# Layer 2 normalizes its attention scores instead of its queries, and the second block's attention runs its last eight units one step later

## The chip, the cores and the metric

The kernel runs on one core of a Trainium2 chip. The metric is the device time of one launch in microseconds; the number given for a kernel is the median of its runs.

## What is computed

Two transformer-like blocks in float32 over 512 tokens of width 1024. The first block has four layers with residual sums; its second layer ("layer 2" here, `mixer_b`) is a dilated window attention. The second block begins with a differential attention over 512 tokens and 256 context tokens. These two are touched:

```python
def mixer_b(h, w_in, q_gain, k_gain, w_out):
    ...
    for g, (window, dilation) in enumerate(B_PATTERNS):     # 3 groups, 8 heads of 128
        q = apply_partial_rotary(rms_norm(qkv[:, :, 0, g], q_gain[g]), cos, sin)
        k = apply_partial_rotary(rms_norm(qkv[:, :, 1, g], k_gain[g]), cos, sin)
        o, lse = dilated_window_attention(q, k, qkv[:, :, 2, g], window // dilation, dilation)
    ...
    y = o.reshape(bsz, S, B_WIDTH) * jax.nn.silu(z)
    return y @ w_out

def diff_attend(q, k, v, lam):                              # 8 heads, 2 maps each
    s = jnp.einsum("bqhpd,bkhpd->bhpqk", q, k) * (HEAD_DIM_2 ** -0.5)
    p = jax.nn.softmax(s, axis=-1)
    a = p[:, :, 0] - lam * p[:, :, 1]
    return jnp.einsum("bhqk,bkhe->bqhe", a, v)
```

`rms_norm` divides by the root of the mean square over a head's 128 features. The partial rotary turns the first 32 features.

## The kernel before

The program is written by hand, engine by engine: `pe_program`, `act_program`, `dve_program`, `pool_program` and `sp_program` each issue their instructions in the order of the code, and semaphores (`wait_ge`, `then_inc`) join them. An engine runs its list strictly in order, so a wait holds up all that stands behind it. Nothing schedules; the order of the loops is the order on the chip. In the names, T and X count TensorE's events, A ScalarE's, V VectorE's and G GpSimd's.

**Products.** A product with a weight keeps float32 accuracy through three matmuls of type fp32r (`mm3`, lines 547 to 549): high part by high part, high by low, low by high. A weight panel is 128 by 2048 float32. SP loads it into one of three slots (`Wr`), ScalarE rounds it to `Wh` (line 1322), GpSimd subtracts to get `Wl` (line 355, four pieces), and `ahead` on both engines does this for the panel two further on. A plain float32 matmul, as for sums of squares, is one instruction that the profile records twice.

**Layer 2.** Features lie on partitions, tokens on columns. For each pair of heads `i` (4 of them) TensorE makes 12 tiles of queries and keys, `t` = 4*group + 2*(key) + head, each of 24 matmuls of 512 columns, then six value tiles, two gate tiles and eight units `u` of attention. After each tile comes `ssq` of the tile before (line 792): a float32 matmul of all ones by the squares, so that each token's sum stands on all 128 partitions. ScalarE squares the tile (line 1518), copies it (line 1523) and takes the root of the sums (line 1510). In `rest`, VectorE inverts the 128x512 roots (line 2133), multiplies tile, gain and inverse (line 2138), swaps halves of 32 rows (line 2147) and multiplies by the sine table (line 2149). GpSimd's `rope` multiplies by the cosine (line 409) and adds (line 412), for queries and keys alike.

A unit is 128 queries by 512 keys: four small matmuls and two large ones into PSUM (lines 832 and 834); VectorE adds the mask and takes the row's maximum in one pass (line 2163) and scales it (line 2166); ScalarE exponentiates (line 1536); VectorE divides (lines 2170 and 2172); TensorE transposes (`flip`, line 843) one unit later; then the products with the values (lines 856 and 863). Each of units 0 to 3 stands behind a value tile, units 4 and 6 behind a gate tile, units 5 and 7 behind none.

**The output projection of layer 2** begins in the last units' tail (`part_out`). ScalarE's `out` first squares two finished output tiles (line 1379), which wait for VectorE's residual sums (line 1967), and then rounds the panel two ahead.

**The second block's attention.** 32 units `g` of 128 queries, eight heads of four. `step(n)` on TensorE issues the scores of unit n+1 (line 1080), the transposes of unit n (`flip`, lines 1090 and 1095) and the product with the values of unit n-1 (line 1111). VectorE's step is `combine(n)` (lines 2348 and 2350), `maxima(n+1)` (lines 2333 and 2335), a copy of two transposed blocks (line 2386) and `weights(n+1)` (lines 2340 and 2342); ScalarE copies the other four blocks (line 1739) and exponentiates both maps (line 1715). The scores of a unit fill PSUM banks 4 to 7, so those of n+1 wait for the exponentials of n. Up to n = 23 each step also holds a projection tile of some 5.8 us. From n = 24 there is none: from n = 25 a step holds two matmuls of a filter (`filt`, line 1150, through PSUM bank 3), which VectorE multiplies (lines 2360 to 2364) and GpSimd adds (lines 454 and 455). After each head come `sums` (line 643), a root, `spread` (line 648) and a scaled copy (lines 2398 and 2002). Then `first_out` starts the output projection.

Of the kernel before, what the change touches and what calls it, by code (L numbers as in the profile page):

```python
# [116 lines left out]

def near_keys(ap, t):

    return ap.rearrange("a (r q n) -> a q r n", r=4, q=4)[:, t:t + 2]  # L120
# [8 lines left out]
D_UNITS = D_HEADS * TT  # L129
FILTER_AT = {25 + 4 * half + t: (half, t) for half in range(2) for t in range(TT)}  # L130
# [67 lines left out]
def setting(nc, ctx, I):  # L198
# [19 lines left out]
    E.ones, E.ident = sb("ones", [P, P]), sb("ident", [P, P])  # L218
# [6 lines left out]
    E.rc = sb("rc", [P, 2, TT])  # L225
    E.rs = sb("rs", [P, 2, S])
    E.sq = sb("sq", [P, 2, S])
# [9 lines left out]
    with ExitStack() as over:  # L237
# [8 lines left out]
            ("stB", [P, B_UNITS, 4], F32), ("PTB", [P, 4, 512], F32), ("szB", [P, S], F32))  # L246
# [15 lines left out]
    E.dlF, E.woF, E.decF, E.kcF = phase(("dlF", [P, D], F32), ("woF", [64, 2 * D], F32), ("decF", [P, 2, S], F32), ("kcF", [P, 2, 2, 512], F32))  # L262
# [17 lines left out]
D_FIRST = [0, 1, 2, 4, 3, 5, 6, 7]  # L280

# [63 lines left out]
def pool_program(E, pool):  # L345
# [39 lines left out]
    def mixer_b():  # L385
        norm("B", E.Ah, E.Al)
        for i in range(4):
            t = 0
            for g in range(3):
                for qk in range(2):  # L390
                    for f in range(2):
                        if t:
                            rope(i, t - 1)
                        if f == 0:
                            ahead("B", "qk", i, g, qk)
                        t += 1
            for g in range(3):
                ahead("B", "v", i, g)
                if g == 0:
                    rope(i, 11)  # L400
            ahead("B", "z", i)
        out("B", 0)

    def rope(i, t):
        g, qk, f = t // 4, t // 2 % 2, t % 2
        q = (E.KB if qk else E.QB)[0:32, g, f, :]
# [121 lines left out]
def pe_program(E, pe):  # L528
# [255 lines left out]
    def mixer_b():  # L784
# [3 lines left out]
        def ssq(i, t):  # L788
            r = t % 2
            into(4 + r)  # L790
            pe.wait_ge(*A.of("B", "sq", i, t))
            pe.matmul(psx[:, r, :], ones[:], sq[:, r, :], start=True, stop=True).then_inc(*X.did("B", "ssq", i, t))  # L792
            emptied[4 + r] = A.of("B", "sqrt", i, t)

        def qk(i, t):
# [11 lines left out]
            if t:  # L807
                ssq(i, t - 1)
# [15 lines left out]
        def scores(i, u):  # L824
# [3 lines left out]
            if r == 0:  # L828
                pe.wait_ge(*G.of("B", "rope", i, 10 + hh))
# [60 lines left out]
        for i in range(4):  # L890
# [5 lines left out]
            ssq(i, 11)  # L896
# [136 lines left out]
    def attention():  # L1033
# [119 lines left out]
        def step(n, f):  # L1153
            if f:
                filt(*f, 0)
            if n + 1 < D_UNITS:
                scores(n + 1)
            if n < D_UNITS:
                flip(n)
            if 1 <= n <= D_UNITS:  # L1160
                values(n - 1)
            if f:
                filt(*f, 1)
            if n >= 5 and (n - 2) % TT == 3:
                sums((n - 2) // TT)
            if n >= 6 and (n - 3) % TT == 3:
                spread((n - 3) // TT)
# [7 lines left out]
        for n in range(D_UNITS + 1):  # L1175
# [137 lines left out]
def act_program(E, act):  # L1313
# [51 lines left out]
    def out(L, half, squares, src, before):  # L1365

        for n in range(4):
            beside = L == "A3" and half
            if beside and n < 2:
                context(n)  # L1370
            if n == 3 and squares and not beside:
# [11 lines left out]
            ahead(L, "o", half, n)  # L1383
# [111 lines left out]
    def mixer_b():  # L1495
        PB, stB, ropeB = E.PB, E.stB, E.ropeB
        qf = E.QB[:].rearrange("p a b n -> p (a b n)")
# [3 lines left out]
        act.dma_start(qf[:, 0:4 * 512], I["k_maskB"]).then_inc(*LDB.did(0))  # L1501
# [3 lines left out]
        def sqrt(i, t):  # L1505
            r = t % 2
            act.wait_ge(*X.of("B", "ssq", i, t))
            if t >= 2:
                act.wait_ge(*V.of("B", "qk", i, t - 2))
            act.activation(rs[:, r, :], psx[:, r, :], ACT.Sqrt, bias=eps[:, 0:1], scale=1.0 / P).then_inc(*A.did("B", "sqrt", i, t))  # L1510

        def qk(i, t):
            act.wait_ge(*T.of("B", "qk", i, t))
            if t >= 2:
# [1136 lines left out]
```

## Time and profile before

| | |
|---|---|
| median of 3 runs | 3177.42 us (3175.05 to 3180.74) |
| the profiled execution, its own time | 3173.78 us |
| its span | 3171.9 us |
| TensorE busy | 3097.2 us, 98% of the span |
| VectorE, GpSimd, ScalarE busy | 1577.5, 1552.7, 1099.8 us |
| mean granted clock of TensorE | 0.992 of full speed |

The profile is one execution. Busy time of TensorE counts from the start of a matmul to a modelled end, and ends of neighbours overlap, so that the time one matmul takes from the others is read from the distance between starts and not from its duration. An idle time is shown with what ended it.

### The profile page before, as it was taken

How to read it: one execution, taken by the hardware profiler on the slowest of the kernel's cores; microseconds unless marked ns; L12 is line 12 of the kernel's file. 1: busy time of each engine (PE TensorE's matmuls, PEld its weight loads, DVE VectorE, ACT ScalarE, POOL GpSimd, SP SyncE). 2: the span in 40 equal slices, each digit the busy share in tenths (PEclk: the TensorE clock that was granted, in tenths of full speed). 3: DMA queues.
4: the chain of work that ended last, by engine and by line, in shares of the span. 5: the costliest groups of instructions: out<-in, count | busy, mean ns of one | idle time of the engine just before them, and what ended most of it. 6: DMA issues, size and time to landing. Idle time of an engine off the chain costs nothing.

```text
span 3171.9 us, 38137 instructions
## 1 busy us (share of the span) xinstructions
PE 3097.2 (98%) x15692; PEld 2524.8 (80%) x15692; DVE 1577.5 (50%) x2066; ACT 1099.8 (35%) x1445; POOL 1552.7 (49%) x1138
## 2 busy tenths in 40 slices
PE   8999999999999999999999999899999999999998
PEld 6888878788887888878887888666888777778887
DVE  6654474838473525355456777644211356542113
ACT  3322244444443423332223444434222343242222
POOL 4444475748473555454434422235544565355444
PEclk9999999999999999999999999999999999999999
DMA  5544322222222323355443111112223242222331
GB/s 199 171 151 159 133 93 70 80 67 80 67 80 68 105 93 95 109 187 176 137 160 116 54 41 41 41 54 93 93 94 106 81 146 81 79 68 93 97 103 67
DMA packets 270975, 319.24 MB, mean 101 GB/s; under 512 B 6851, under 2 KB 228690, under 8 KB 270483
## 3 DMA queue, kind: packets, MB, share of 16 engines
q1 hardware_dynamic: 232768, 247.48, 24.2%
q10 hardware_dynamic: 38034, 69.34, 6.4%
q8 instruction: 124, 2.03, 0.3%
q14 instruction: 49, 0.39, 0.0%
HBM read 310.50 MB, written 6.29 MB: 100 GB/s over the span
## 4 chain that ended last, share of the span: by engine, by line
PE 92%; DVE 4%; ACT 1%; POOL 1%; issue 1%; DMA 1%; ACTq 0%; SPq 0%; DVEq 0%
PE ps L547 26%; PE ps L549 25%; PE ps L548 25%; PE psx L792 1%; PE psx L1080 1%; PE ps L1111 1%; PE ps L618 1%; PE psx L771 1%; POOL Wl L355 1%; PE psx L1234 1%; PE ps L586 1%; DVE stD L2333 1%; PE psx L834 1%; PE ps L582 1%; PE ps L583 1%
## 5 line engine op out<-in xcount | busy, mean ns | idle before, releaser
L355 POOL TENSOR_TENSOR Wl<-Wr,Wh 128x512 fp32r<-128x512 f32 x928 | 1269.7, 1400 | 1415.7 <-ACT Wh L1322 1411.5
L547 PE MATMUL ps<-Ah,Wh 128*128 128x512 f32 x1944 | 778.1, 400 | 0.0
L549 PE MATMUL ps<-Ah,Wl 128*128 128x512 f32 x1944 | 757.5, 390 | 0.0
L548 PE MATMUL ps<-Al,Wh 128*128 128x512 f32 x1944 | 757.3, 390 | 0.0
L1322 ACT ACTIVATE Wh<-Wr 128x2048 fp32r<-128x2048 f32 x232 | 443.0, 1909 | 354.7 <-DMA Wr<-in_w_mlp_in_dram 110.2
L547 PEld LDWEIGHTS ps<-Ah,Wh 128*128 128x128 f32 x1944 | 365.1, 188 | 84.9 <-issue 12.0
L547 PE MATMUL ps<-Yh,Wh 128*128 128x512 f32 x1088 | 426.8, 392 | 5.2 <-POOL Wl L355 5.2
L548 PEld LDWEIGHTS ps<-Al,Wh 128*128 128x128 f32 x1944 | 365.2, 188 | 82.1 <-issue 8.9
L549 PEld LDWEIGHTS ps<-Ah,Wl 128*128 128x128 f32 x1944 | 364.9, 188 | 77.0
L548 PE MATMUL ps<-Yl,Wh 128*128 128x512 f32 x1088 | 424.5, 390 | 0.0
L549 PE MATMUL ps<-Yh,Wl 128*128 128x512 f32 x1088 | 424.3, 390 | 0.0
L547 PEld LDWEIGHTS ps<-Yh,Wh 128*128 128x128 f32 x1088 | 205.1, 188 | 50.0 <-POOL Wl L355 5.6
L549 PEld LDWEIGHTS ps<-Yh,Wl 128*128 128x128 f32 x1088 | 204.9, 188 | 42.9
L548 PEld LDWEIGHTS ps<-Yl,Wh 128*128 128x128 f32 x1088 | 205.0, 188 | 42.2
L547 PE MATMUL ps<-Wh,Ah 128*128 128x256 f32 (+1 forms) x688 | 220.7, 321 | 2.1 <-DVE vA L2057 2.1
L548 PE MATMUL ps<-Wl,Ah 128*128 128x256 f32 (+1 forms) x688 | 215.1, 313 | 0.0
L549 PE MATMUL ps<-Wh,Al 128*128 128x256 f32 (+1 forms) x688 | 215.0, 313 | 0.0
L2049 DVE SCALAR_TENSOR_TENSOR macc<-modw,sc,macc 128x512 f32<-128x512 f32 x168 | 158.4, 943 | 111.1 <-DMA modw<-in_w_mod_dram 104.6
L2133 DVE RECIPROCAL rs<-rs 128x512 f32<-128x512 f32 x48 | 160.6, 3346 | 38.9 <-ACT rs L1510 38.9
L2410 DVE TENSOR_TENSOR tmp<-tmp 128x512 f32<-128x512 f32 x64 | 52.3, 817 | 201.2 <-ACT tmp L1786 201.2
L547 PEld LDWEIGHTS ps<-Wh,Ah 128*128 128x128 f32 x688 | 131.1, 191 | 13.8 <-issue 4.3
L548 PEld LDWEIGHTS ps<-Wl,Ah 128*128 128x128 f32 x688 | 131.1, 191 | 9.2 <-issue 1.9
(404 smaller groups left out, 3895.6 us busy)
## 6 DMA issues: line engine op xcount, KB each, us to landing
Wr<-in_a_w_in_dram SPq DMA_DIRECT2D x48, 1024.0 KB, 6.6
modw<-in_w_mod_dram ACTq DMA_DIRECT2D x96, 512.0 KB, 5.5
Wr<-in_b_w_in_dram SPq DMA_DIRECT2D x40, 1024.0 KB, 5.0
Wr<-in_w_mlp_in_dram SPq DMA_DIRECT2D x32, 1024.0 KB, 5.5
Wr<-in_w_mlp_out_dram SPq DMA_DIRECT2D x32, 1024.0 KB, 5.1
Wr<-in_a_w_out_dram SPq DMA_DIRECT2D x16, 1024.0 KB, 5.1
Wr<-in_c_w_in_dram SPq DMA_DIRECT2D x16, 1024.0 KB, 5.5
Wr<-in_attn_w_qkv_dram SPq DMA_DIRECT2D x12, 1024.0 KB, 5.1
```

What stands on the lines that cost most here:

```text
L355: last = pool.tensor_tensor(E.Wl[:, s, part], E.Wr[:, s, part], E.Wh[:, s, part].bitcast(F32), ALU.subtract)
L547: pe.matmul(o, ah, bh, start=first, stop=False)
L548: pe.matmul(o, ah, bl, start=False, stop=False)
L549: return pe.matmul(o, al, bh, start=False, stop=last)
L582: pe.matmul(bank[b], part(E.Wh, p, k, f * P, f * P + P, KD), Ah[:, k, :], start=(k == 0), stop=False)
L583: pe.matmul(bank[b], part(E.Wl, p, k, f * P, f * P + P, KD), Ah[:, k, :], start=False, stop=False)
L586: m = pe.matmul(bank[b], part(E.Wh, p, k, f * P, f * P + P, KD), Al[:, k, :], start=False, stop=(k == KD - 1))
L618: pe.matmul(bank[t], Ah[:, a, t * P:(t + 1) * P], part(W, p, k, 0, S, TT), start=(a == 0 and W is E.Wh), stop=False)
L1322: act.activation(E.Wh[:, s, :], E.Wr[:, s, :], ACT.Copy).then_inc(*HI.did(p))
L2049: dve.scalar_tensor_tensor(t, w, E.sc2[:, k, who:who + 1], t, ALU.mult, ALU.add).then_inc(*V.did("mac", L, nb, who, k))
L2133: dve.reciprocal(rs[:, r, :], rs[:, r, :]).then_inc(*V.did())
L2410: dve.tensor_tensor(t, t, t, ALU.mult).then_inc(*V.did(L, "sqr", iq, c))
```

## The change

**Early rounding.** In ScalarE's `out` of layer 2 the first `ahead` stands ahead of the first two squares.

**Queries of layer 2.** ScalarE writes the tile times its gain straight into `QB`. The sums of squares of both heads' query tiles come from eight float32 matmuls of 32 output rows and 128 columns, ScalarE takes roots of 128x256, TensorE transposes them in two 128x128 blocks, so that a token's root stands in a column, and VectorE inverts four columns of each. The scores are multiplied by that column in the pass that adds the mask, which is now three instructions (one per group of the three attentions) and a maximum of its own. The rotation of queries is wholly on VectorE: shuffle, two products, one sum, of 32 rows each.

**Keys of layer 2.** Squares are rounded by ScalarE to `rsR`, VectorE takes the rest `sqR`, and the sum is two fp32r matmuls. Roots, 128x512 inverses, gain and rotation stay as before.

**Later order.** From unit 24 on, the transposes of unit n-1 and the values of n-2 stand in step n; VectorE's step begins with `maxima(n+1)`, and `combine(n)` comes after the first filter product. From unit 25 the second map's weights alternate between two buffers. There is one more step, and the two last heads' sums come one step later.

The core of the diff:

```diff
+D_LAST = 24
+def is_key(t):
+    return t // 2 % 2 == 1
+def second(E, g):
+    return E.p1E[:] if g > D_LAST and g % 2 else E.p1D
+def behind(h):
+    return 1 if 4 * h >= D_LAST else 0
...
 # pe_program, mixer_b
-        def ssq(i, t):
-            r = t % 2
-            into(4 + r)
-            pe.wait_ge(*A.of("B", "sq", i, t))
-            pe.matmul(psx[:, r, :], ones[:], sq[:, r, :], start=True, stop=True).then_inc(*X.did("B", "ssq", i, t))
+        def key_sum(i, t):
+            b = 5 - t % 2
+            into(b)
+            pe.wait_ge(*V.of("B", "sl", i, t))
+            pe.matmul(bank[b], E.onesR[:], E.rsR[:, t % 2, :], start=True, stop=False)
+            pe.matmul(bank[b], E.onesR[:], E.sqR[:, t % 2, :], start=False, stop=True).then_inc(*X.did("B", "ssq", i, t))
+        def query_sums(i, g):
+            into(4)
+            pe.wait_ge(*A.of("B", "sq", i, 4 * g + 1))
+            for f in range(2):
+                for q in range(TT):
+                    m = pe.matmul(psx[32 * q:32 * q + 32, 0, f * P:(f + 1) * P], ones[:, 0:32], sq[:, f, q * P:(q + 1) * P], start=True, stop=True)
+        def columns(i, g):
+            pe.wait_ge(*A.of("B", "sqrt", i, 4 * g))
+            for f in range(2):
+                m = pe.transpose(psx[:, 0, (2 + f) * P:(3 + f) * P], rs[:, 1, f * P:(f + 1) * P], ident[:])
-            if t:
-                ssq(i, t - 1)
+            if t % 4 == 2:
+                query_sums(i, t // 4)
+            elif t % 4 == 3:
+                key_sum(i, t - 1)
+                columns(i, t // 4)
+            elif t % 4 == 0 and t:
+                key_sum(i, t - 1)
...
 # dve_program, mixer_b
+        def turn_query(i, t):
+            q, swapped = QB[0:32, t // 4, t % 2, :], PB[0:32, 0, :]
+            dve.wait_ge(*A.of("B", "cp", i, t))
...
+            dve.stream_shuffle(swapped, q, SWAP).then_inc(*V.did())
+            dve.tensor_tensor(swapped, swapped, ropeB[:, 1, :], ALU.mult).then_inc(*V.did())
+            dve.tensor_tensor(q, q, ropeB[:, 0, :], ALU.mult).then_inc(*V.did())
+            dve.tensor_tensor(q, q, swapped, ALU.add).then_inc(*V.did("B", "turned", i, t))
...
-            dve.tensor_tensor_reduce(PB[:, u % 2, :], psx[:, u % 2, :], maskB[:, u % 4, :], 1.0, 10 * NEG,
-                                     ALU.add, ALU.max, stB[:, u, 0:1]).then_inc(*V.did("B", "sc", i, u))
+            for g, c0, c1 in ((0, 0, 256), (1, 256, 384), (2, 384, 512)):
+                dve.scalar_tensor_tensor(PB[:, u % 2, c0:c1], psx[:, u % 2, c0:c1], rq(g, u // 4)[:, u % 4:u % 4 + 1], maskB[:, u % 4, c0:c1],
+                                         ALU.mult, ALU.add).then_inc(*V.did("B", "sc", i, u))
+            dve.tensor_reduce(stB[:, u, 0:1], PB[:, u % 2, :], AX.X, ALU.max).then_inc(*V.did("B", "mx", i, u))
...
-            for t in range(11):
-                rest(i, t)
+            for t in range(13):
+                if t % 4 == 3:
+                    rate(i, t // 4)
+                if t < 12:
+                    if is_key(t):
+                        square_low(i, t)
+                    else:
+                        turn_query(i, t)
+                if t and is_key(t - 1):
+                    scaled(i, t - 1)
+                    turn_key(i, t - 1)
...
 # act_program, out
+            if L == "B" and n == 0:
+                ahead(L, "o", half, n)
...
-            ahead(L, "o", half, n)
+            if L != "B" or n:
+                ahead(L, "o", half, n)
...
 # pe_program, attention
         def step(n, f):
+            late = n >= D_LAST
+            if n + 1 < D_UNITS:
+                scores(n + 1)
             if f:
                 filt(*f, 0)
-            if n + 1 < D_UNITS:
-                scores(n + 1)
-            if n < D_UNITS:
+            if not late:
                 flip(n)
-            if 1 <= n <= D_UNITS:
+            elif D_LAST <= n - 1 < D_UNITS:
+                flip(n - 1)
+            if 1 <= n <= D_LAST:
                 values(n - 1)
+            elif D_LAST <= n - 2 < D_UNITS:
+                values(n - 2)
             if f:
                 filt(*f, 1)
...
 # dve_program, attention: the order within a late step
+            if late and n + 1 < D_UNITS:
+                maxima(n + 1)
...
+            g = n - 1 if late else n
...
             if n in FILTER_AT:
                 filt(*FILTER_AT[n], 0)
+            if late and n < D_UNITS:
+                combine(n)
+            if n in FILTER_AT:
+                filt(*FILTER_AT[n], 1)
             if n + 1 < D_UNITS:
                 weights(n + 1)
```

**How the order moves.** On TensorE, layer 2, head pair 0, behind a tile. Before, the float32 sum:

```order
L548 MATMUL ps<-Al,Wh 128x512
L549 MATMUL ps<-Ah,Wl 128x512
L792 MATMUL psx<-sq,ones 128x512
L547 MATMUL ps<-Ah,Wh 128x512
L548 MATMUL ps<-Al,Wh 128x512
```

and now, behind the second key tile of a group:

```order
L567 MATMUL ps<-Al,Wh 128x512
L568 MATMUL ps<-Ah,Wl 128x512
L811 MATMUL psx<-rsR,onesR 128x512
L812 MATMUL psx<-sqR,onesR 128x512
L827 MATMUL psx<-ident,rs 128x128 x2
L566 MATMUL ps<-Ah,Wh 128x512
```

The one float32 sum became two fp32r matmuls, and the transposes of the queries' roots stand behind them. Behind the first key tile of a group stand the eight small matmuls (line 820) instead, behind the next group's first query tile the two of the second key tile, and behind a second query tile nothing.

On ScalarE, where layer 2's output projection begins (`Wh` is a rounded weight panel). Before:

```order
L1598 ACTIVATE Yh<-sq 128x512
L1546 ACTIVATE PTB<-psx 128x512 x2
L1598 ACTIVATE Yh<-szB 128x512
L1379 ACTIVATE sq<-x 128x512 x2
L1322 ACTIVATE Wh<-Wr 128x2048
L1379 ACTIVATE sq<-x 128x512 x2
L1322 ACTIVATE Wh<-Wr 128x2048
```

and now:

```order
L1670 ACTIVATE Yh<-sq 128x512
L1614 ACTIVATE PTB<-psx 128x512 x2
L1670 ACTIVATE Yh<-szB 128x512
L1369 ACTIVATE Wh<-Wr 128x2048
L1428 ACTIVATE sq<-x 128x512 x4
L1369 ACTIVATE Wh<-Wr 128x2048
```

The rounding of the panel stands right behind the last head's `Yh`, ahead of the squares.

On TensorE in the attention's tail (`psx<-KD,QD` are scores, `ps<-ident,PD` transposes, `ps<-tmp,VD` values, `ps<-woF,hdX` filter matmuls). Before:

```order
L1150 MATMUL ps<-woF,hdX 128x512
L648 MATMUL ps<-ident,rc 128x128 x4
L1150 MATMUL ps<-woF,hdX 128x512
L1080 MATMUL psx<-KD,QD 128x512 x2
L1080 MATMUL psx<-KD,QD 128x256 x2
L1090 MATMUL ps<-ident,PD 128x128 x4
L1095 MATMUL ps<-ident,PD 128x128 x2
L1111 MATMUL ps<-tmp,VD 128x128 x6
```

and now:

```order
L667 MATMUL ps<-ident,rc 128x128 x4
L1121 MATMUL psx<-KD,QD 128x512 x2
L1121 MATMUL psx<-KD,QD 128x256 x2
L1191 MATMUL ps<-woF,hdX 128x512
L1131 MATMUL ps<-ident,PD 128x128 x4
L1136 MATMUL ps<-ident,PD 128x128 x2
L1152 MATMUL ps<-tmp,VD 128x128 x6
L1191 MATMUL ps<-woF,hdX 128x512
```

The scores moved ahead of the step's first filter matmul. The transposes and values read alike in both lists, but now belong to the units one earlier, as the diff shows.

## Rows read from the trace of the kernel before

**Rows 1.** The page: busy us, share of the span and instructions of each engine.

```profile
PE 3097.2 (98%) x15692; PEld 2524.8 (80%) x15692; DVE 1577.5 (50%) x2066; ACT 1099.8 (35%) x1445; POOL 1552.7 (49%) x1138
```

**Rows 2.** Windows of layer 2 and of the tail: length, busy per engine, PE clock.

```profile
421.00:993.00 572.00, 570.72 (x3361) 472.41 (x3362) 355.10 (x433) 248.17 (x378) 359.55 (x256) 1.00 0.23 74
2025.80:2096.57 70.77, 56.97 (x277) 37.73 (x277) 50.05 (x74) 32.83 (x58) 20.12 (x14) 0.90 0.05 14
```

**Rows 3.** Timeline of PE in layer 2's projections: start us, duration, line, tile.

```profile
440.18 1.02 PE L792 MATMUL psx<-sq,ones 128*128 128x512 f32 x2
...
441.27 0.40 PE L548 MATMUL ps<-Al,Wh 128*128 128x512 f32 x1
...
446.52 1.02 PE L792 MATMUL psx<-sq,ones 128*128 128x512 f32 x2
```

**Rows 4.** Timeline of PE in the preamble, a sum of squares in tiles of 32 columns.

```profile
18.95 0.43 PE L667 MATMUL psx<-sq,ones 128*32 128x128 f32 x8
19.30 0.66 PE L698 MATMUL ps<-ident,stage 128*128 128x128 f32 x4
```

**Rows 5.** Timeline of PE in layer 2's units 4 and 5, head block 0.

```profile
533.66 0.60 PE L843 MATMUL psx<-ident,PB 128*128 128x128 f32 x4
534.10 1.06 PE L856 MATMUL ps<-tmp,VB 128*128 128x128 f32 x8
...
536.64 0.63 PE L843 MATMUL psx<-ident,PB 128*128 128x128 f32 x4 [0.28 <-DVE PB L2172]
```

**Rows 6.** Timeline of DVE in the same units.

```profile
534.04 0.69 DVE L2163 CUSTOM_DVE_ANT_0 PB<-psx,maskB 128x512 f32<-128x512 f32 x1 [4.67 <-PE psx L834]
...
534.78 0.15 DVE L2166 TENSOR_SCALAR stB<-stB 128x1 f32<-128x1 f32 x1
```

**Rows 7.** Groups of layer 2 (420 to 993 us): busy us, mean ns, idle before.

```profile
L2133 DVE RECIPROCAL rs<-rs 128x512 f32<-128x512 f32 x48 | 160.6, 3346 | 38.9 <-ACT rs L1510 38.9
...
L2138 DVE SCALAR_TENSOR_TENSOR QB<-tmp,PK,rs 128x512 f32<-128x512 f32 x24 | 26.1, 1087 | 0.9
...
L2149 DVE TENSOR_TENSOR tmp<-tmp,ropeB 32x512 f32<-32x512 f32 x24 | 17.0, 707 | 0.8
...
L2147 DVE STREAM_SHUFFLE tmp<-KB 32x512 f32<-32x512 f32 x12 | 8.8, 730 | 0.1
```

**Rows 8.** Timeline of ACT, POOL and PE where layer 2's output projection runs.

```profile
991.09 0.63 ACT L1598 ACTIVATE Yh<-szB 128x512 fp32r<-128x512 f32 x1 [6.71 <-DVE szB L2178]
...
997.53 1.90 ACT L1322 ACTIVATE Wh<-Wr 128x2048 fp32r<-128x2048 f32 x1
...
999.52 10.83 POOL L355 TENSOR_TENSOR Wl<-Wr,Wh 128x512 fp32r<-128x512 f32 x8 [28.31 <-ACT Wh L1322]
...
1005.44 0.79 PE L547 MATMUL ps<-Yh,Wh 128*128 128x512 f32 x1 [5.17 <-POOL Wl L355]
...
1009.39 0.40 PE L547 MATMUL ps<-Yh,Wh 128*128 128x512 f32 x1
```

**Rows 9.** Timeline of PE in the attention's tail, units 24 to 31.

```profile
2025.80 2.30 PE L1080 MATMUL psx<-KD,QD 64*128 64x512 f32 x8 [3.02 <-ACT rs L1715]
...
2032.26 1.56 PE L1080 MATMUL psx<-KD,QD 64*128 64x512 f32 x8
...
2034.94 1.50 PE L1111 MATMUL ps<-tmp,VD 128*128 128x128 f32 x12
...
2073.76 0.75 PE L1080 MATMUL psx<-KD,QD 64*128 64x512 f32 x1
...
2087.29 0.63 PE L1090 MATMUL ps<-ident,PD 128*128 128x128 f32 x4 [3.66 <-DVE PD L2350]
...
2096.57 0.50 PE L547 MATMUL ps<-Yh,Wh 128*128 128x512 f32 x1
```

**Rows 10.** Timeline of DVE in the tail.

```profile
2028.14 1.76 DVE L2333 TENSOR_REDUCE stD<-psx 128x2 f32<-128x1536 f32 x1 [0.49 <-PE psx L1080]
...
2033.09 1.02 DVE L2350 SCALAR_TENSOR_TENSOR PD<-PD,stD,rs 128x768 f32<-128x768 f32 x1
```

More of the change, by code:

```diff
@@ L225, in setting @@
     E.rc = sb("rc", [P, 2, TT])
+    E.rsR, = phase(("rsR", [P, 2, S], F32R))
     E.rs = sb("rs", [P, 2, S])
+    E.sqR, = phase(("sqR", [P, 2, S], F32R))
     E.sq = sb("sq", [P, 2, S])
@@ L1174, in attention @@
         scores(0)
-        for n in range(D_UNITS + 1):
+        for n in range(D_UNITS + 2):
             if n < 24:
@@ L1729, in attention @@
         exp(0, 1)
-        for n in range(D_UNITS + 3):
+        for n in range(D_UNITS + 4):
             if n < 24:
@@ L2014, in preamble @@
     def preamble():
[L2015 removed]
+        dve.memset(E.acc[:], 1.0).then_inc(*V.did())
+        dve.wait_ge(*V.now())
+        dve.tensor_copy(E.onesR[:], E.acc[:, 0:P]).then_inc(*V.did("ones"))
         dve.memset(eps[:], EPS).then_inc(*V.did("eps"))
@@ L2125, in mixer_b, with square_low, rq, rate @@
         dve.wait_ge(*E.signals["ld_b"].of(1))
-        dve.tensor_copy(maskB[:].rearrange("p r n -> p (r n)"), QB[:].rearrange("p a b n -> p (a b n)")[:, 0:4 * 512]).then_inc(*V.did("mask"))
+        dve.tensor_copy(maskB[:].rearrange("p r n -> p (r n)"), KB[:].rearrange("p a b n -> p (a b n)")[:, 0:4 * 512]).then_inc(*V.did("mask"))
         dve.wait_ge(*V.of("mask"))
-        def rest(i, t):
-            g, qk, f, r = t // 4, t // 2 % 2, t % 2, t % 2
-            dst = (KB if qk else QB)[:, g, f, :]
+        def square_low(i, t):
+            r = t % 2
+            dve.wait_ge(*A.of("B", "sh", i, t))
+            dve.tensor_tensor(E.sqR[:, r, :], sq[:, r, :], E.rsR[:, r, :].bitcast(F32), ALU.subtract).then_inc(*V.did("B", "sl", i, t))
+        def rq(g, f):
+            return stB[:, B_UNITS + 2 * g + f, :]
+        def rate(i, g):
+            dve.wait_ge(*X.of("B", "rt", i, g))
+            for f in range(2):
+                dve.reciprocal(rq(g, f), psx[:, 0, (2 + f) * P:(3 + f) * P].rearrange("p (q n) -> p q n", q=TT)[:, :, 0]).then_inc(*V.did("B", "rq", i, g))
+        def scaled(i, t):
+            n, r = t // 4 * 2 + t % 2, t % 2
             dve.wait_ge(*A.of("B", "sqrt", i, t))
@@ L2369, in attention @@
         weights(0)
-        for n in range(D_UNITS + 3):
-            if n < D_UNITS:
+        for n in range(D_UNITS + 4):
+            late = n >= D_LAST
+            if late and n + 1 < D_UNITS:
+                maxima(n + 1)
+            if not late:
                 combine(n)
@@ L2375, in attention @@
                 tile(n // 8 + 1, n % 8)
-            if n + 1 < D_UNITS:
+            if not late:
                 maxima(n + 1)
+            if n < 24 and not copied:
+                tile(n // 8 + 1, n % 8)
+            g = n - 1 if late else n
+            if n != D_LAST and g < D_UNITS:
+                dve.wait_ge(*X.of("D", "f1", g))
+                if g >= 2:
+                    dve.wait_ge(*X.of("D", "pv", g - 2))
+                dve.tensor_copy(tmp[:, 2 * (g % 2) + 1, 0:256], ps[1][:, 0:256]).then_inc(*V.did("D", "e1", g))
```

208 lines of the change are left out of this document (116 added, 92 removed).

## The prediction

> **What bounds the kernel.** I read the page first: TensorE is busy for 98% of the span [rows 1], so that time can come only from work taken off TensorE or from its few stalls, and busy time of another engine counts only where TensorE waits for it. The windows come next [rows 2]. In layer 2, from 421 to 993 us, TensorE is busy for 570.7 of 572.0 us at full clock. In the attention's tail, from 2025.8 to 2096.6 us, it is busy for 57.0 of 70.8 us, and the granted clock is 0.90. There both waits and slow stretches are to be had. Last come the timelines of these places, for prices, and the groups of VectorE in layer 2, for whether it keeps up.
>
> **Layer 2, the sums of squares.** From 441.27 to 446.52 us TensorE starts 23 matmuls of 512 columns, 0.228 us each [rows 3]. From the start of a float32 sum (440.18) to that of the second matmul behind it (441.27) are 1.09 us; less the first of the two, the sum costs 0.86 us. 48 such sums are 41.3 us, all on the path. The order shows what stands in their place.
> - Keys: 24 times two fp32r matmuls, 0.46 us a pair, 10.9 us. The pace is that of `mm3`, which has the same types.
> - Queries: 12 times eight matmuls of 128 columns into 32 rows. Four of this very form take 0.35 us from their start to the next instruction [rows 4]; one after another they would take 0.86. So I take 0.70 us for eight. The ends are 0.43 (two quarters of 0.86, nothing lost) and 1.72 (no overlap).
> - Two transposes behind them: four take 0.44 us [rows 5], so 0.22 for two.
>
> That is 10.9 + 12 x 0.92 = 21.9 us against 41.3: **19.4 us less**.
>
> The four small matmuls of rows 4 have 128-column tiles on both sides, so the row holds both changes of mode. The Trainium skill (TensorEngine Tiling, Key Properties) says that a change of tiling mode drains TensorE, which speaks against this edit. If each of 12 groups paid another 0.35 us for it, the gain here would be 15.2 us; the row says it is paid already.
>
> **Layer 2, VectorE's load.** Today four tiles ask of it 4 x (3.35 + 1.09 + 0.73 + 0.71) = 23.5 us [rows 7], beside 25.4 us of TensorE (4 x 6.34) [rows 3]. Afterwards: two inverses 6.7, two products with the gain 2.2, four shuffles 2.9, eight products or sums of 32 rows 5.7, two rests of squares at 1.09 (the nearest form, 128x512 from SBUF), inverses of columns 0.4: 20.1 us. TensorE's four tiles take 4 x 24 x 0.228 + 0.92 + 0.92 = 23.7 us. So VectorE keeps up on average. TensorE newly waits for it at each key sum (`sl`). The tightest is the first key tile of a group: ahead of its rest of squares stand the two inverses of the group before and the next two query rotations. Laid end to end from the roots of that group, they finish some 1.4 us ahead of TensorE. I price this wait at nothing and keep 1 us at each of 8 places (groups 1 and 2, four head pairs) for the range. GpSimd loses half its rotations, ScalarE gains a rounding per key tile and loses half of its wide roots; both have idle time behind a tile, so nothing.
>
> **Layer 2, the units.** Mask and maximum take 0.89 us from start to scaled maximum [rows 6]. In their place come pieces of 256, 128 and 128 columns and a maximum over 512. A row of 512 columns from PSUM takes 0.69 and one of one column 0.15, so in proportion 0.42 + 0.28 + 0.28, less some overlap 0.85; the maximum 0.69, the scaling 0.15, hand-overs 0.1: 1.8 us, or **0.9 more**. The ends are 0.3 more (pieces at 0.69 in all, maximum 0.5) and 2.5 more (each piece as dear as a full row). A unit with a value or gate tile behind it hides this under 5.5 us. Only unit 5 has none: its transposes of unit 4 already wait 0.28 us [rows 5]. So four times 0.9, **3.6 us more** (1.2 to 10).
>
> **Early rounding.** TensorE waits 5.17 us for GpSimd at 1005.44, and the nine matmuls behind it take 3.95 us, until 1009.39, in place of 2.05: 7.1 us [rows 8]. The rounding that GpSimd waited for started at 997.53, behind two squares. It can now start at 991.7, right behind `Yh`, end at 993.6, and GpSimd's four pieces (10.83 for eight) end at 999.0; TensorE wants the panel at 1000.3. So **7.1 us less**. What is late next is the panel after it, whose rounding stays behind four squares and now has 7 us less to come: GpSimd's second four pieces end at 1010.35 in the old order, and TensorE now wants them at 1000.3 plus 48 matmuls, 1011.2. So nothing, by 0.9 us. The squares move by nothing, since the rounding is over when the first residual sum is.
>
> **The tail.** One unit's loop, which no order can shorten: from the start of the maximum (2028.14) over the exponentials to the next scores (2032.26) 4.1 us, and the scores themselves 1.56, with a hand-over 5.8 us [rows 9, 10]. Today the combination of two maps (`combine`, 1.7 us on VectorE, its longer part 1.02) stands ahead of the maximum and ahead of the transposes that TensorE waits for, once for 3.66 us. The last scores start at 2073.76, so six loops took 48 us, 8.0 each. With the new order the combination is beside the exponentials. Six loops make 34.6 us. To these come 0.8 us, since the second map of unit 25 waits for the combination of 24, now behind a maximum, 0.7 for the sums of head 5 and 2.3 for its scaled copy ahead of a maximum: last scores at 2025.8 + 38.4 = 2064.2, plus 0.7 for the first scores, which run slow: 2064.9. Behind them the old order takes 22.8 us. The new one loses the wait of 3.7 and, as I estimate from the window's clock of 0.90, 2 us of slow matmuls, and has one set of transposes (0.6) and one product with the values (1.5) more [rows 9]: some 19 us, end at 2083.9, 12.7 less. Hand-overs that I left out are some 0.2 us in eight steps: **11 us less**. Ends: 3 less (VectorE's 50 us [rows 2] and the filter's bank set an uneven pace) and 15 less (all idle time gone).
>
> **Sum** against the profiled execution of 3173.78 us (span 3171.9): 19.4 - 3.6 + 7.1 + 11 = 33.9 us less, 3139.9. The median of the runs is 3.6 us above that execution; from 3177.42 the forecast is **3143.5 us**.
>
> **Rivals.**
> - *The tail stays uneven*: the last step's filter product and the head's scaled copy on VectorE each hold up a maximum, and the gain is 3 us. For: VectorE's work there is 50 us for eight steps, 6.3 each, more than the loop's 5.8. Against: part of it is contention at today's places. 3151.5.
> - *VectorE late in layer 2*: 8 waits of 1 us at the key sums, none hidden. For: only 1.4 us to spare. 3151.5.
> - *The small matmuls do not run side by side* in this place, so the change does not do what it should for queries: 12 x 1.02 = 12.2 us back, 3155.7. Against: rows 4.
> - *Slower: VectorE becomes layer 2's engine.* The rotation products beside GpSimd's `Wl` pieces stretch. The gain of 33.9 us is gone when a group of four tiles takes 2.8 us more than TensorE's 23.7, that is, when the eight narrow ones take 1.5 in place of 0.71. At 1.8 us each the group takes 28.8, 5.1 x 12 = 61 us: 3204. For: the 128x512 product with the gain means 1.09 us, more than the 0.69 of rows 6. Against: the 32-row product stands at 0.71 beside the same GpSimd work [rows 7]. The Trainium skill (GPSIMD Engine Reference, Key points) says that GpSimd shares its SBUF interfaces with VectorE where an instruction has two SBUF inputs, as all these have.
>
> **Numbers.** Forecast 0.60; tail uneven 0.14; VectorE late 0.12; no overlap 0.05; better than forecast, near 3135 (the tail at its upper end, unit 5 at its lower), 0.06; slower 0.03. The range 3134 to 3158 takes in all but the last and the mixed corners. 0.2% (6.4 us) is about what a measurement tells from no change: faster 0.95, same 0.02, slower 0.03.
>
> **What would show it.** Behind a key tile, starts of `psx<-rsR` and the next `mm3` matmul 0.46 us apart, without a wait for `sqR`; the eight small ones 0.7 us; unit 5's transposes waiting 1.2 us; no wait for `Wl` near 990 us; scores in the tail 5.8 to 6.5 us apart. The forecast is wrong if TensorE's waits for VectorE in layer 2 pass 10 us, or if the tail, from unit 25's scores to the output projection, takes over 65 us.

## The result and the profile after

The changed kernel takes **3198.06 us** (median of 5 runs, 3190.30 to 3202.18) against 3177.42 for the kernel before (5 runs): ratio 1.0061, 95% interval 1.0045 to 1.0078. That is 20.6 us slower, where 33.9 us less were forecast, and outside the range. The profiled execution took 3190.3 us (span 3188.6).

The page of the changed kernel, against [rows 1]: TensorE is busy for 9 us less, in a span 16.7 us longer.

```profile
PE 3088.2 (97%) x15860; PEld 2526.0 (79%) x15860; DVE 1621.4 (51%) x2179; ACT 1108.1 (35%) x1457; POOL 1494.2 (47%) x1090
```

To find the place I took one mark per stage, the transposes that spread a norm. First four rows of the kernel before (PE timeline), then the same four of the changed kernel: the entry and the exit of layer 2, and two marks around the attention's tail.

```profile
405.38 1.16 PE L648 MATMUL psx<-ident,rc 128*128 128x128 f32 x8
1033.57 1.11 PE L648 MATMUL psx<-ident,rc 128*128 128x128 f32 x8
2012.34 1.06 PE L648 MATMUL ps<-ident,rc 128*128 128x128 f32 x8
2104.41 1.05 PE L648 MATMUL psx<-ident,rc 128*128 128x128 f32 x8
```

```profile
407.16 1.16 PE L667 MATMUL psx<-ident,rc 128*128 128x128 f32 x8
1057.46 1.11 PE L667 MATMUL psx<-ident,rc 128*128 128x128 f32 x8
2037.47 1.06 PE L667 MATMUL ps<-ident,rc 128*128 128x128 f32 x8
2122.32 1.05 PE L667 MATMUL psx<-ident,rc 128*128 128x128 f32 x8
```

The mark's start is the first number of each row. Layer 2 went from 628.2 to 650.3 us, **22.1 more**, where 22.9 less were forecast (19.4 - 3.6 + 7.1). The tail went from 92.1 to 84.9 us, 7.2 less where 11 were forecast. All other stages together moved by 1.8 us. So layer 2 missed by 45.0 us, and nearly the whole error is there.

The waits of TensorE in layer 2 (405 to 1057 us), with the engine, the line, what released it, us in total, times and the longest:

```profile
PE psx L811 <- DVE sqR L2207: 32.3, 8, 6.5
PE psx L884 <- DVE PB L2277: 4.5, 4, 1.1
```

The key sums wait for VectorE's rest of squares at eight places, 32.3 us in all: five waits of 5.9 to 6.5 us (31.0 in all) and three of 0.4 to 0.6. The PE timeline around the first long wait, ahead of key tile 6:

```profile
457.85 0.39 PE L568 MATMUL ps<-Ah,Wl 128*128 128x512 f32 x1
464.76 0.77 PE L811 MATMUL psx<-rsR,onesR 128*128 128x512 f32 x1 [6.52 <-DVE sqR L2207]
...
468.31 0.63 PE L568 MATMUL ps<-Ah,Wl 128*128 128x512 f32 x1
468.74 0.63 PE L566 MATMUL ps<-Ah,Wh 128*128 128x512 f32 x1
...
473.27 0.39 PE L811 MATMUL psx<-rsR,onesR 128*128 128x512 f32 x1
473.50 0.39 PE L812 MATMUL psx<-sqR,onesR 128*128 128x512 f32 x1
473.73 0.39 PE L566 MATMUL ps<-Ah,Wh 128*128 128x512 f32 x1
```

TensorE stands for 6.52 us, and then its starts are 0.43 us apart in place of 0.23 until 469.6: the 1.2 GHz level. From the start at 464.76 to the next key sum at 473.27 are 8.51 us, where the same matmuls take 6.14 in run 5 below, which has no such wait: another 2.4 us. Behind each of the five long waits the clock is low for some microseconds. The window of all of layer 2 and that of one of the slow stretches follow (after the window and its length stand the busy times of PE, PEld, DVE, ACT and POOL, then the clock):

```profile
421.00:1001.00 580.00, 542.65 (x3399) 458.55 (x3399) 383.34 (x526) 249.53 (x378) 300.36 (x208) 0.97 0.22 71
...
938.00:945.00 7.00, 6.92 (x34) 6.66 (x35) 4.39 (x5) 3.50 (x4) 0.00 (x0) 0.57 0.01 2
```

Why was VectorE late? Its groups in layer 2, against [rows 7] (busy us, mean ns):

```profile
L2248 DVE TENSOR_TENSOR QB<-QB,ropeB 32x512 f32<-32x512 f32 x24 | 59.6, 2482 | 0.0
L2250 DVE TENSOR_TENSOR QB<-QB,PB 32x512 f32<-32x512 f32 x24 | 31.9, 1329 | 0.8
L2207 DVE TENSOR_TENSOR sqR<-sq,rsR 128x512 fp32r<-128x512 f32 x24 | 26.8, 1117 | 10.7 <-ACT rsR L1582 10.7
...
L2247 DVE TENSOR_TENSOR PB<-PB,ropeB 32x512 f32<-32x512 f32 x24 | 18.2, 760 | 0.8
```

The sine product (L2247) costs 0.76 us as counted. The cosine product (L2248), of the same shape, costs 2.48 and the sum (L2250) 1.33. The timelines of DVE and POOL at the first of the worst places:

```profile
443.83 0.68 DVE L2247 TENSOR_TENSOR PB<-PB,ropeB 32x512 f32<-32x512 f32 x1
444.44 6.77 DVE L2248 TENSOR_TENSOR QB<-QB,ropeB 32x512 f32<-32x512 f32 x1
451.24 0.68 DVE L2250 TENSOR_TENSOR QB<-QB,PB 32x512 f32<-32x512 f32 x1
```

```profile
442.07 1.79 POOL L428 TENSOR_TENSOR KB<-KB,ropeB 32x512 f32<-32x512 f32 x1 [3.91 <-DVE tmp L2234]
443.94 1.71 POOL L431 TENSOR_TENSOR KB<-KB,tmp 32x512 f32<-32x512 f32 x1
445.63 5.04 POOL L374 TENSOR_TENSOR Wl<-Wr,Wh 128x512 fp32r<-128x512 f32 x4
```

A product of 0.68 us of work took 6.77. It started while GpSimd was in a rotation's sum, and it ended 0.55 us after the sum and the four `Wl` pieces behind it were over. GpSimd has a wait ahead of the pieces, for ScalarE's `Wh`, but it was met by then, so GpSimd never stood still between them. Five of the 24 cosine products are like this (6.67 to 6.77 us), one for each long wait; the rest of squares stands behind them in VectorE's order. These five are the long holds below.

### The profile page after: what moved, and what is told of

The parts are those of the page before. It is cut to its first block, busy times and chain, and to the rows that moved or that the text cites. A ratio compares the mean times of both kernels' runs of the same rounds, so it can differ in the third digit from the quotient of the medians.

```text
span 3188.6 us, 38480 instructions
## 1 busy us (share of the span) xinstructions
PE 3088.2 (97%) x15860; PEld 2526.0 (79%) x15860; DVE 1621.4 (51%) x2179; ACT 1108.1 (35%) x1457; POOL 1494.2 (47%) x1090
## 4 chain that ended last, share of the span: by engine, by line
PE 87%; DVE 8%; issue 2%; ACT 1%; POOL 1%; DMA 1%; ACTq 0%; SPq 0%; DVEq 0%
PE ps L566 24%; PE ps L567 24%; PE ps L568 24%; DVE QB L2248 1%; PE psx L1121 1%; PE ps L637 1%; PE ps L1152 1%; PE psx L790 1%; DVE rs L2220 1%; PE psx L1281 1%; PE psx L875 1%; PE ps L605 1%; DVE stD L2446 1%; PE psx L873 1%; PE ps L601 1%
## 5 line engine op out<-in xcount | busy, mean ns | idle before, releaser
L566 PE MATMUL ps<-Ah,Wh 128*128 128x512 f32 x1944 | 768.8, 395 | 1.2 <-DVE vA L2132 1.2
L568 PEld LDWEIGHTS ps<-Wh,Al 128*128 128x128 f32 x688 | 132.1, 192 | 7.7
```

The costliest lines, as they stand in the source:

```text
L566: pe.matmul(o, ah, bh, start=first, stop=False)
L568: return pe.matmul(o, al, bh, start=False, stop=last)
```

## The experiments

Every ratio below is against runs of the kernel before on the same chip: 3174.7 us for runs 1, 2, 5 and 6, 3175.8 for runs 3 and 7 to 9, 3174.2 for runs 4 and 10 to 12. The chips differ between these groups, so times of different groups are compared by their ratios.

**1. A wait between the two products.** My first theory was that VectorE's own order makes the hold: a second product that starts straight behind a first.

```diff
             dve.tensor_tensor(swapped, swapped, ropeB[:, 1, :], ALU.mult).then_inc(*V.did())
+            dve.wait_ge(*V.now())
             dve.tensor_tensor(q, q, ropeB[:, 0, :], ALU.mult).then_inc(*V.did())
```

> The changed kernel with one wait more: the queries' cosine product waits for the sine product before it to end, so no product of the rotation is started right behind another. Theory A (a VectorE product that starts directly behind another one, while GpSimd goes from a rotation's sum straight into a panel's four low pieces, is held until the pieces end; five of them, 6.7 us each; each makes TensorE wait 6.2 us and then run 6.8 us at the 1.2 GHz level, which costs 3.4 more, so 5 x 9.6 = 48): no product over 2 us is left, TensorE's wait for sqR falls from 32.3 us to under 2, and the time is 3198 - 48 = 3150. Rival B (the hold comes from where GpSimd stands, not from how VectorE starts): the five products stay at 6 to 7 us and the time at 3198. Rival C (VectorE's load in layer 2 is too high anyway): the long products go, the waits for sqR stay above 20 us, 3185 to 3200.

Measured: 3194.46 us, ratio 1.0064 (1.0052 to 1.0077). Four of the five cosine products are held as before (6.65 or 6.66 us), and TensorE still waits 28.5 us for `sqR`:

```profile
443.57 6.65 DVE L2249 TENSOR_TENSOR QB<-QB,ropeB 32x512 f32<-32x512 f32 x1
```

Theory A falls: the held products no longer start straight behind another one. The fifth, at the last place, was not held this time; there GpSimd happened to stand still for 0.66 us behind its sum, waiting for `Wh`.

**2. Gaps between GpSimd's pieces.**

```diff
             last = pool.tensor_tensor(E.Wl[:, s, part], ...)
+            if c < 1536 and E.at["B", "qk", 0, 0, 0] <= p < E.at["B", "o", 0, 0]:
+                last.then_inc(*G.did("piece", p, c))
+                pool.wait_ge(*G.of("piece", p, c))
```

> The changed kernel, but in layer 2 GpSimd waits for each of a panel's four low pieces to end before it starts the next, so its stream has gaps in it. Theories A and B both say that a held product of VectorE then gets in after one piece: none over 2 us, waits for sqR under 2 us, 3150 to 3155. Rival C: 3185 to 3200, and the waits stay. If the product is still held over four pieces, the hold is no matter of the gap between GpSimd's instructions: 3198.

Measured: 3190.64 us, 1.0049 (1.0036 to 1.0062). The same place in this run, DVE and then POOL:

```profile
449.20 3.01 DVE L2251 TENSOR_TENSOR QB<-QB,ropeB 32x512 f32<-32x512 f32 x1
```

```profile
448.76 1.64 POOL L434 TENSOR_TENSOR KB<-KB,tmp 32x512 f32<-32x512 f32 x1
450.38 6.06 POOL L374 TENSOR_TENSOR Wl<-Wr,Wh 128x512 fp32r<-128x512 f32 x4
```

Now the hold lasts over the sum and the first piece, between which GpSimd still does not stand still, and ends at the first gap. So the length of the hold is GpSimd's to set (theory B). Four products are held for 3.01 us, none for longer. But the expectation of 3150 to 3155 failed: the waits for `sqR` are still 21.0 us in all, a wait of 3.9 us for the norm ahead of layer 2 has come in, and the time is only some 4 us lower by the ratios. The long hold is not all.

**3. One gap, ahead of the pieces.**

```diff
         pool.tensor_tensor(q, q, spare, ALU.add).then_inc(*G.did("B", "rope", i, t))
+        pool.wait_ge(*G.of("B", "rope", i, t))
```

> The changed kernel, with one gap in GpSimd's stream: it waits for a rotation's sum to end before it goes to the panel's low pieces; the four pieces themselves follow each other as before. Theory B (a VectorE product of two SBUF inputs waits for a gap in GpSimd's stream, and the long holds come where sum and pieces follow without one): the product that starts in the sum gets in at its end, no product over 2 us, the waits for sqR fall from 32 us to about 20 us as in the run with gaps between the pieces, and the time to about 3188. Rival D (it is the pieces' own stream that holds, whatever stands ahead of it): the five products stay at 6 to 7 us, 3195 to 3200.

Measured: **3176.51 us**, 0.9999 (0.9991 to 1.0008), level with the kernel before. One wait instruction on GpSimd takes back about 20 us (ratio 1.0061 to 0.9999). No cosine product is over 1.78 us now. The timelines at the same place, DVE and POOL, and the waits left in layer 2:

```profile
443.24 1.76 DVE L2249 TENSOR_TENSOR QB<-QB,ropeB 32x512 f32<-32x512 f32 x1
445.03 1.67 DVE L2251 TENSOR_TENSOR QB<-QB,PB 32x512 f32<-32x512 f32 x1
...
454.50 1.77 DVE L2249 TENSOR_TENSOR QB<-QB,ropeB 32x512 f32<-32x512 f32 x1
456.30 1.66 DVE L2251 TENSOR_TENSOR QB<-QB,PB 32x512 f32<-32x512 f32 x1
```

```profile
442.74 1.71 POOL L431 TENSOR_TENSOR KB<-KB,tmp 32x512 f32<-32x512 f32 x1
444.53 5.83 POOL L374 TENSOR_TENSOR Wl<-Wr,Wh 128x512 fp32r<-128x512 f32 x4
```

```profile
PE psx L812 <- DVE sqR L2208: 16.0, 8, 2.8
```

Thirteen cosine products start inside a GpSimd sum here, five of them 0.48 to 0.50 us into it as at 444.44, and none is held on: behind each of these sums GpSimd now stands still, mostly for 0.08 us. Rival D falls, and theory B is shown in both directions. I had expected 3188, since the run with four gaps stood there. What makes this run better than that one was not tried further. The traces show that there the cosine products mean 1.61 us and the sums 1.68, here 1.50 and 1.58, and that the wait of 3.9 us for the norm is gone.

**4. The rest of squares earlier.** With the gap of run 3, which this run keeps, eight waits remain, six of 2.4 to 2.8 us and two of 0.4. Is VectorE too busy (rival C), or only late at one point (theory E)?

```diff
+                if t < 12 and t % 4 == 1:
+                    square_low(i, t + 1)
                 if t < 12:
-                    if is_key(t):
+                    if t % 4 == 3:
                         square_low(i, t)
-                    else:
+                    elif not is_key(t):
                         turn_query(i, t)
```

> The changed kernel with the one gap (3176.5; 16 us of waits for sqR left, eight of about 2 us), and on VectorE the rest of a first key tile's squares ahead of the second query's rotation instead of behind it. No work changes its engine; only the order in which TensorE's partner takes it. Theory E (VectorE is not too busy over the stretch, it is late at this one point because two queries' rotations of 5 us each stand ahead of the rest): the waits go, with them the slow clock (10 us at half speed), 3176.5 - 16 - 5 = 3155. Rival C (VectorE's work exceeds TensorE's over four tiles): the waits move to the second key tile's rest or to the scores, and 3168 or more remains.

Measured: **3154.78 us**, 0.9928 (0.9916 to 0.9940), as theory E had it, with 0.8 us of waits for `sqR` left:

```profile
PE psx L812 <- DVE sqR L2208: 0.8, 2, 0.4
```

Nothing was moved off VectorE. Its cosine products and sums still mean 1.45 and 1.67 us, and it keeps up, though with little to spare. In a stretch of four tiles, from one set of query sums to the next, it is busy for 22.9 of 23.8 us (the third busy time):

```profile
591.20:614.99 23.79, 23.79 (x119) 19.24 (x118) 22.89 (x24) 10.92 (x15) 18.04 (x11) 1.00 0.27 89
```

Rival C falls.

**5. Cosine product and sum on GpSimd.** The column scale and the fp32r sums stay.

```diff
+                rope(i, 4 * g)
...
+                rope(i, 4 * g + 1)
...
-            dve.tensor_tensor(q, q, ropeB[:, 0, :], ALU.mult).then_inc(*V.did())
-            dve.wait_ge(*V.now())
-            dve.tensor_tensor(q, q, swapped, ALU.add).then_inc(*V.did("B", "turned", i, t))
```

> The changed kernel with the queries' cosine product and the rotation's sum on GpSimd again, as in the kernel before; VectorE keeps the shuffle and the sine product. Theories A and B: VectorE has no two products in a row left, no product over 2 us, the waits for sqR go, and GpSimd has 24 x 2 x 1.5 us more but is at 52 per cent of the stretch now: 3150, as low as with the wait. Rival C: VectorE's load falls by 24 x 1.4 us = 34 us here too, so it also gives about 3150 to 3160; what tells the two apart is the run with the wait. If GpSimd comes late with the last rotation, the first scores of a head pair wait for it: some us more.

Measured: **3153.37 us**, 0.9931 (0.9919 to 0.9944), without any wait for `sqR`. Layer 2, between the same two marks, takes 605.3 us, 22.9 us less than in the kernel before; the forecast's terms make 22.9. Holds are not gone: six products of tile, gain and inverse take 3.4 us beside GpSimd's pieces, but nothing of TensorE waits for them.

**6. The keys' sums in float32 again,** in the changed kernel.

```diff
-            pe.wait_ge(*V.of("B", "sl", i, t))
-            pe.matmul(bank[b], E.onesR[:], E.rsR[:, t % 2, :], start=True, stop=False)
-            pe.matmul(bank[b], E.onesR[:], E.sqR[:, t % 2, :], start=False, stop=True)...
+            pe.wait_ge(*A.of("B", "sq", i, t))
+            pe.matmul(bank[b], ones[:], sq[:, t % 2, :], start=True, stop=True)...
```

> The changed kernel, but the keys' sums of squares are one float32 product again that waits for the square alone; the rounded squares, their rests and the waits for VectorE are gone, the queries' part stays. The held products stay (theory A, B), but nothing of TensorE waits for VectorE in the tiles any more: the waits for sqR (32.3 us) and the slow clock behind them (17 us) go, and 24 x 0.4 us of the keys' gain are given back: 3198 - 48 + 10 = 3160. Rival C (VectorE late anyway): ScalarE then waits for tmp and rs to come free, TensorE for its banks, by 20 us or more: 3180 or above.

Measured: 3162.59 us, 0.9961 (0.9947 to 0.9974). The time is near the expected 3160, but one part of the expectation failed: the long holds did not stay, and no cosine product is over 1.78 us. Eight of them do start inside a GpSimd sum, but behind each of these sums GpSimd stands still for 0.14 to 0.18 us, waiting for `Wh`, so this fits theory B. But this run does not show what a long hold costs when no key sum waits behind it. What runs 5 and 6 show together is that the loss needs both edits, the rotation on VectorE and the key sum that waits for VectorE: with either one alone the kernel is faster than before.

**7 to 9. What the parts are worth** in the kernel of run 5. Run 7 leaves out the later order, run 8 the early rounding, and run 9 takes float32 sums of the keys.

> The version with the queries' cosine product and sum on GpSimd (3153.4 before), without the later order of the last attention units. The trace of the changed kernel has this stretch at 63.6 us where the kernel before has 70.8. If that 7.2 us is what the order is worth, 3160.5; if it is worth the 12.7 us of the forecast's count, 3166; if the slower clock or later waits take it back elsewhere, 3153 to 3156.

> The version with the queries' cosine product and sum on GpSimd (3153.4), without the early rounding of the first output panel. With the forecast's 5.17 us of wait and 1.9 us of slow clock the time rises to 3160.5. If GpSimd now comes to this panel in time by itself, it stays at 3153 to 3155; if only the wait comes and the clock stays, 3158.5.

> The version with the queries' cosine product and sum on GpSimd (3153.4), with the keys' sums of squares as one float32 product again. TensorE pays 24 x (0.86 - 0.46) = 10 us more by the forecast's figures; if the keys' wait for VectorE is free in this version (no such wait in its trace), the time is 3163.4. If the rests and the second product cost TensorE more than they save, 3153 or less.

Without the early rounding (run 8): 3156.95 us (ratio 0.9936, 0.9924 to 0.9949); between the marks of layer 2 it is 7.1 us longer, and the wait of 5.1 us for `Wl` is back. With float32 sums of the keys (run 9): 3158.49 us (0.9945, 0.9931 to 0.9958); between the marks 9.7 us longer. Without the later order (run 7): 3152.13 us (0.9929, 0.9916 to 0.9941), no slower than with it, though the trace has the tail 5.3 us longer. All three intervals overlap that of run 5, so the three prices rest on one trace each and the timed runs do not resolve them; 3160.5, 3160.5 and 3163.4 had been expected of runs 7, 8 and 9.

**10 to 12. The tail, and a small wait.** The first also puts `far(i, 2)` ahead of `flip(i, 4)`; the second is the same without the later order; the third is the kernel before with the later order alone.

```diff
+                if n == 5:
+                    far(i, 2)
                 if 1 <= n < 7:
                     flip(i, n - 1)
...
                 elif n == 5:
-                    far(i, 2)
                     far(i, 3)
```

> The version with the queries' cosine product and sum on GpSimd (3153.4), and in each head pair the value products of unit 2 put between the scores of unit 5 and the transposes of unit 4, which wait there 1.1 us for VectorE (4.5 us in all by that version's trace). If that wait is covered: 3149, and no wait for PB left. If the wait only moves to the next step (VectorE's weights of unit 5): 3153.

> The version just named (value products of unit 2 ahead), without the later order of the last attention units, on the same chip. The first such pair gave 3153.4 with the order and 3152.1 without, where the traces gave 5.3 us for it, with 27 us of the stretch at the 1.2 GHz level with the order and 24 without. Theory T1 (the order is worth 5 to 8 us and the first pair's runs hid it in their scatter): 3154 to 3157, against 3149 with it. Theory T2 (the clock takes it back): as fast as with it, within 2 us.

> The kernel before with the later order of the last attention units alone, layer 2 and the output panel as they were. Theory T1: 3175.8 - 7 = 3169, and in its trace some 7 us less from the norm spread at 2012 us to the one at 2104 us. Theory T2: 3174 to 3177, with more of the stretch at the 1.2 GHz level.

Measured, in this order: **3148.06 us** (0.9911, 0.9899 to 0.9924), the lowest median of all, though its interval overlaps that of run 5; its wait for `PB` fell from 4.5 to 2.7 us, not to none. The same without the later order: 3148.97 us (0.9924, 0.9911 to 0.9936). The later order alone on the kernel before: 3168.18 us (0.9982, 0.9973 to 0.9991), 6 us faster, as T1 said. Between the marks of the tail it is worth 7.2 us in the changed kernel, 6.3 alone, 5.3 in run 5 and 2.0 in the last pair. The eleven traces with it have 83.6 to 90.8 us there, the three without it 92.1, 92.7 and 96.1. The windows from unit 25's scores to the output projection, in run 5 and in the changed kernel, have nearly the same work of VectorE, and differ in the clock:

```profile
2003.69:2073.22 69.53, 61.34 (x276) 39.25 (x277) 50.93 (x75) 31.54 (x56) 17.92 (x15) 0.80 0.05 14
```

```profile
2050.94:2114.49 63.55, 55.63 (x276) 35.34 (x277) 50.60 (x75) 31.64 (x56) 17.93 (x15) 0.90 0.05 14
```

So the order shortens the tail in every pair of traces, by 2.0 to 7.2 us, and the stretch is 6 us longer where the clock is 0.80 than where it is 0.90. That the clock makes all of this difference is not shown. In two pairs of timed runs the gain is inside their scatter; only the pair on the kernel before resolves it.

## Why the prediction was wrong

**The sums of squares: right.** From the start of the eight small matmuls (427.76) to the second matmul behind them are 0.91 us; less the first of the two, as the forecast counted the float32 sum, they cost 0.68 where 0.70 was counted, so no change of mode costs more here than rows 4 had in it. A key pair costs 0.46 (473.27 to 473.73). The keys' part, counted at 24 x 0.40 = 9.6 us, came out at 9.7 in run 9.

**Unit 5: right.** Its four waits make 4.5 us where 1.1 stood before, 3.4 more against 3.6.

**Early rounding: right** between the marks of layer 2, 7.1 us (run 8). The medians of the timed runs differ by 3.6 us, inside their scatter.

**VectorE's load: this step failed,** and with it the pricing of the key sums' wait "at nothing". It counted "eight products or sums of 32 rows 5.7", 0.71 us each, from the row of the kernel before. But of those 48 products 19 start 0.04 or 0.05 us ahead of a GpSimd instruction, and the other 29 start 0.16 to 0.18 us before one ends, so that none meets GpSimd in the middle of something. These rows of the kernel before, DVE and then POOL, were there to be read:

```profile
458.04 1.67 DVE L2138 SCALAR_TENSOR_TENSOR QB<-tmp,PK,rs 128x512 f32<-128x512 f32 x1
...
460.67 0.68 DVE L2149 TENSOR_TENSOR acc<-acc,ropeB 32x512 f32<-32x512 f32 x1
```

```profile
457.88 1.27 POOL L412 TENSOR_TENSOR QB<-QB,tmp 32x512 f32<-32x512 f32 x1
460.71 1.79 POOL L409 TENSOR_TENSOR QB<-QB,ropeB 32x512 f32<-32x512 f32 x1 [1.56 <-DVE acc L2147]
```

At 460.67 VectorE is first by 0.04 us; it takes its 0.68, and GpSimd's product takes 1.79 in place of 1.28. At 458.04 GpSimd is first by 0.16, and VectorE's product takes 1.67, where the quickest of its group take 0.75. So the price depends on who is first, and the four new instructions of a group (two cosine products, two sums) mostly come when GpSimd is already at work: in run 3, 40 of the 48 take 1.65 to 1.78 us and eight 0.68, not 0.71. All four stand ahead of a first key tile's rest of squares. In the rows of run 3 they take 1.76, 1.67, 1.77 and 1.66, 4.0 us more than counted, where the forecast had 1.4 to spare; that leaves 2.6, and six of the eight waits of run 3 are 2.4 to 2.8 us. The load as a whole was undersized too, 20.1 us for four tiles where run 4 has 22.9, but that is still under TensorE's 23.8. The other half, the hold of 6.77 us over several GpSimd instructions, no row of the kernel before has (in layer 2 its longest product is 1.88 us), and it was not foreseen in any rival.

The sum: layer 2 came out 45.0 us above its terms, and also 45.0 above run 5, which has the same matmuls without these waits. The starts of the key sums in the two traces split this up: 32.3 us are the waits for `sqR`, 1.3 the starts behind them (0.16 for each of the eight), and 10.7 the matmuls at the 1.2 GHz level behind the five long ones (1.7 to 2.7 each, 2.4 in the rows at 464.76). The rest is 0.7 us.

**The rival that ended slower** had the mechanism, that the rotation's products stretch beside GpSimd's pieces, and the forecast's own limit of 10 us of waits in layer 2 was passed (32.3). It had the size and the place wrong: it priced a load that exceeds TensorE's over the whole stretch, 61 us. Run 4 shows that the load can be carried; what broke was one deadline. Its chance of 0.03 leaned on the mean of 0.71 us. The rival "VectorE late in layer 2" had the place right, the same eight key sums, and priced each at 1 us: 8 us in all, where 45.0 were lost.

**The tail: the mechanism right, the size not.** From unit 25's scores to the output projection it is 63.6 us where 58.1 was counted (59.8 with the allowance for hand-overs) and 70.8 stood before. The loops make nearly all of the difference. Six of them with their extras were counted at 39.1 us and took 44.3: the first four 7.3 to 8.4 us, the last two 6.3, where the bare loop was counted at 5.8. At two of the scores, 2050.94 and 2066.90, the clock was at the 1.2 GHz level (granted clock 0.50 from 2050.0 to 2056.8 and from 2063.6 to 2070.4), and they take 2.93 us in place of 1.56. PE starts of the scores (waits in brackets), then VectorE through one such loop:

```profile
2050.94 2.93 PE L1121 MATMUL psx<-KD,QD 64*128 64x512 f32 x8 [3.02 <-ACT rs L1789]
...
2058.80 1.56 PE L1121 MATMUL psx<-KD,QD 64*128 64x512 f32 x8 [2.07 <-ACT p1E L1789]
...
2066.90 2.93 PE L1121 MATMUL psx<-KD,QD 64*128 64x512 f32 x8
...
2075.29 1.56 PE L1121 MATMUL psx<-KD,QD 64*128 64x512 f32 x8
...
2082.55 1.56 PE L1121 MATMUL psx<-KD,QD 64*128 64x512 f32 x8
...
2088.89 1.56 PE L1121 MATMUL psx<-KD,QD 64*128 64x512 f32 x8
...
2095.23 1.56 PE L1121 MATMUL psx<-KD,QD 64*128 64x512 f32 x8
```

```profile
2083.61 1.25 DVE L2455 TENSOR_TENSOR stD<-stD 128x1 f32<-128x1 f32 x1
2084.78 1.75 DVE L2446 TENSOR_REDUCE stD<-psx 128x2 f32<-128x1536 f32 x1
```

And POOL at this place:

```profile
2083.58 1.26 POOL L473 TENSOR_TENSOR hsF<-kcF 128x512 f32<-128x512 f32 x1 [5.89 <-DVE stD L2453]
```

From 2082.6 to 2095.2 VectorE has no idle time, so in the last two loops its work sets the pace. The rival "tail uneven" had this number, 50 us for eight steps, 6.3 each, though as a mean over all steps, and it priced the gain at 3 us where 7.2 came. What holds up the first four loops beyond the slow scores was not taken apart. A good microsecond of it is again a held instruction: a product of one column, 0.16 us at 2050.92, takes 1.25 ahead of the maximum when GpSimd has started 0.03 us before it.

## What to carry to other kernels

Before you give VectorE an instruction with two SBUF inputs, look at what GpSimd is doing when it will start, and price it from rows that start while GpSimd is already at work, not from the group's mean: here 0.71 by the mean, 1.7 by such rows, 6.8 at worst. Where such work cannot be avoided, put what TensorE waits for ahead of it in VectorE's order (run 4), and try a gap in GpSimd's stream ahead of a long run (run 3). Where TensorE stands for 6 us, as at five places here, look at the clock behind it too: it cost another 1.7 to 2.7 us each time.

## What the hardware showed that I had not expected

A VectorE product was held not for one GpSimd instruction but over several between which GpSimd does not stand still: sum and four pieces (6.77 us), sum and one piece where the pieces had waits between them (3.01), the sum alone where GpSimd waited for its end (1.76). It is not only the rotation's products: in run 5 a product of tile, gain and inverse at 584.18 takes 3.40 us, until 0.56 us after the last of GpSimd's pieces. The Trainium skill (SBUF — State Buffer, Who interferes with whom) says that a VectorE instruction with two SBUF inputs contends with a GpSimd instruction that reads SBUF. The same page of the Trainium skill (SBUF: two separate sides) says that of such two the one that starts first has the shared port pair for its whole instruction while the other blocks. The trace agrees for single instructions (1.67 and 1.79 in the rows of the kernel before), and shows that a hold can outlast the instruction. It does not always: at 459.54 a cosine product that starts 0.40 us into a sum, with pieces right behind, gets in at the seam and takes 1.74 us, while the one at 444.44 started 0.50 us into its sum and was held on. The distance alone does not decide it: the one at 929.94 also started 0.40 us into a sum and was held for 6.67 us. What decides it is open.
